# The MLP products of a hybrid decoder layer, as seven-product block multiplications over two token halves

## What is computed

```python
    x = x + gt1 * mix
    h = _rmsnorm(x, g2n) * (1 + sc2) + sh2
    x = x + gt2 * (jnp.square(jax.nn.relu(h @ w_up)) @ w_down)
...
y_prompt = _rmsnorm(xp, g_final)
y_sample = _rmsnorm(xs, g_final)
```

## Time and profile before

| | us |
|---|---|
| median of 3 runs (1808.34 to 1810.19) | 1808.41 |
| span of the profiled execution | 1804.3 |
| TensorE busy (matmuls) | 1775.4 |
| VectorE busy | 759.9 |
| ScalarE busy | 489.3 |
| GpSimd busy | 12.3 |

### The profile page before, as it was taken

One profiled execution on the slowest core, in us unless ns is written; L12 is line 12 of the kernel. 1 busy time (PEld: TensorE's weight loads), 2 busy tenths in 40 slices (PEclk: granted clock), 3 DMA queues, 4 the chain that ended last, 5 costly groups with the idle time before them and its releaser, 6 DMA issues.

```text
span 1804.3 us, 26783 instructions
## 1 busy us (share of the span) xinstructions
PE 1775.4 (98%) x10976; PEld 1713.8 (95%) x10976; DVE 759.9 (42%) x1445; ACT 489.3 (27%) x832; POOL 12.3 (1%) x25
## 2 busy tenths in 40 slices
PE   8999999999999999999999989999999999999997
PEld 3899999999999999999999989999999999999997
DVE  3644324444544545333353564343333333433345
ACT  5443333223333233211232341212121121212122
POOL 0000000000000000000000010000000000000000
PEclk9999999999999999999999989999999999999999
DMA  9444544322331232211132111111111111111112
GB/s 310 141 138 156 176 130 131 83 60 69 88 97 54 63 98 58 58 47 46 49 88 79 47 36 47 48 48 46 46 37 45 46 46 46 46 46 46 47 47 97
DMA packets 192677, 139.34 MB, mean 77 GB/s; under 512 B 15323, under 2 KB 176007, under 8 KB 192630
## 3 DMA queue, kind: packets, MB, share of 16 engines
q1 hardware_dynamic: 185910, 130.01, 24.4%
q10 hardware_dynamic: 6720, 8.67, 1.4%
HBM read 120.86 MB, written 17.80 MB: 77 GB/s over the span
## 4 chain that ended last, share of the span: by engine, by line
PE 95%; DVE 2%; DMA 1%; issue 1%; ACT 1%; SPq 0%; DVEq 0%; ACTq 0%
PE PB L916 85%; PE M L844 3%; PE M L969 1%; PE M L860 1%; PE M L1044 1%; DMA araw<-in_w_ada 1%; PE M L1050 1%; PE M L1036 1%; PE M L1038 1%; DVE XL L1223 1%; PE M L908 0%; PE M L1014 0%; DVE R L1709 0%; ACT A L532 0%; PE M L1061 0%
## 5 line engine op out<-in xcount | busy, mean ns | idle before, releaser
L916 PE MATMUL PB<-XH,whi 128*128 128x352 f32 x2496 | 811.3, 325 | 4.1 <-DVE XL L1223 2.1
L916 PE MATMUL PB<-XH,wlo 128*128 128x352 f32 x2496 | 801.5, 321 | 0.0
L916 PE MATMUL PB<-XL,whi 128*128 128x352 f32 x2496 | 801.3, 321 | 0.0
L916 PEld LDWEIGHTS PB<-XH,whi 128*128 128x128 f32 x2496 | 469.0, 188 | 11.3 <-issue 6.9
L916 PEld LDWEIGHTS PB<-XL,whi 128*128 128x128 f32 x2496 | 470.2, 188 | 0.7
L916 PEld LDWEIGHTS PB<-XH,wlo 128*128 128x128 f32 x2496 | 468.7, 188 | 0.0
L550 ACT ACTIVATE whi<-raw 128x1024 fp32r<-128x1024 f32 x134 | 141.3, 1054 | 407.4 <-PE PB L916 404.3
L916 PE MATMUL PB<-AH,whi 128*128 128x352 f32 x720 | 233.1, 324 | 0.2 <-issue 0.2
L916 PE MATMUL PB<-AL,whi 128*128 128x352 f32 x720 | 232.5, 323 | 0.0
L916 PE MATMUL PB<-AH,wlo 128*128 128x352 f32 x720 | 232.1, 322 | 0.0
L1228 DVE TENSOR_TENSOR wlo<-raw,whi 128x1024 fp32r<-128x1024 f32 x134 | 163.7, 1222 | 118.0 <-ACT whi L550 117.1
(11 more groups left out here) (297 smaller groups left out, 1199.4 us busy)
## 6 DMA issues: line engine op xcount, KB each, us to landing
raw<-in_w_in SPq DMA_DIRECT2D x64, 512.0 KB, 4.8
araw<-in_w_ada SPq DMA_DIRECT2D x48, 512.0 KB, 5.3
raw<-in_w_up SPq DMA_DIRECT2D x32, 512.0 KB, 4.0
raw<-in_w_down SPq DMA_DIRECT2D x32, 512.0 KB, 3.4
zp_d<-zr ACTq DMA_DIRECT2D x16, 512.0 KB, 2.7
Z<-zp_d SPq DMA_DIRECT2D x8, 1024.0 KB, 5.8
xin<-in_x_prompt SPq DMA_DIRECT2D x8, 512.0 KB, 7.0
CU<-in_state_C SPq DMA_DIRECT2D x8, 512.0 KB, 3.8
```

Source lines behind the costliest of these rows:

```text
L916: ins = pe.matmul(PB[:, bank, 0:BLK], w[:, w0:w0 + P], x[:, k, a0:a1], start=(k == 0 and j == 0), stop=(k == n_k - 1 and j == 2))
```

## The change

Both products of the MLP become block multiplications of 2x2 blocks with seven products in place of eight, in Winograd's form with its shared sums. The blocks: two halves of the tokens (`HALF` = 528), two halves of the inner dimension, two halves of a strip of 256 output features.

- **Up**: 16 steps p, each for 256 hidden features: seven products of four k tiles, each with three matmuls for each of two quarters of 264 tokens (`SUB`), in two PSUM banks (`acc`). The two quarters alternate with the same weight tile. Four pairs of banks serve the seven products (`ACC`); three products accumulate on what another left.
- **Down**: 32 steps, four for each of 8 groups of 512 hidden features, seven products of two k tiles.
- **Weights**: of each step seven operands are split; three of them, and the seventh, are sums and differences of the raw blocks, four operations on GpSimd (`sums`, `last_sum`).
- **Combining**: VectorE adds the accumulators (`u2`, `v1`, `t22`, `t21`, `t12`), ScalarE copies the first out (`s1_copy`) and takes relu and square of the four blocks, 528 wide. For the down products four of their seven x operands are differences of the blocks: four chained subtractions on GpSimd (`x_sums`). All seven are split again (high on ScalarE, low on VectorE) and stored to DRAM (`xd_d`), 528 KB each, since they don't fit into SBUF; SyncE loads them again, fourteen for each group, while the group before is multiplied.
- **Norm**: all seven x operands of the up products must be made once, 28 pieces of 528 tokens. The sum of squares is taken by a matmul with a matrix of ones, so that it is spread at once, and the square root (ScalarE) and the reciprocal (VectorE) are taken of 352 columns. Products of step 0 run in the order `FIRST` and wait for their pieces. x itself is stored to DRAM in phase 4 (`xm_d`) and loaded again in the down stage.
- **End**: VectorE and GpSimd combine the halves in the last group; the nine groups of rows are transposed, normed and stored after the last product.

The core of the diff:

```diff
+HALF = T // 2
+SUB = HALF // 2
+LPH = TP - HALF
+UP, DOWN = 16, 32
+ACC = (0, 1, 2, 3, 0, 2, 3)
+XPOS = (1, 5, 4, 3, 2, 6, 0)
+FIRST = (0, 4, 2, 1, 3, 5, 6)
...
+    def acc(a):
+        return PS[:, 2 * a:2 * a + 2, 0:SUB]
...
+        def store_x(p, i, done):
+            sp.wait_ge(s["xl5"], 7 * p + done)
+            sp.dma_start(xd_d[bass.ds(p, 1), :, i + 1, :].rearrange("o p n -> (o p) n"),
+                         XS[:, XPOS[i]].rearrange("p x n -> p (x n)")).then_inc(xbo if done <= 3 else xto, 16)
+        def store_t(p):
+            store_x(p, 3, 4)
+            store_x(p, 2, 5)
+            store_x(p, 1, 6)
+            store_x(p, 5, 7)
...
+        def load_xd(g, b, i, free):
+            sp.wait_ge(s["pd5"], free)
+            sp.wait_ge(xbo, 48 * (2 * g + 2 if isinstance(g, int) else UP))
+            sp.wait_ge(xto, 64 * (2 * g + 2 if isinstance(g, int) else UP))
+            for k in range(2):
+                sp.dma_start(xd(b, i)[:, k].rearrange("p x n -> p (x n)").bitcast(F32),
+                             xd_d[bass.ds(2 * g + k, 1), :, i + 1, :].rearrange("o p n -> (o p) n")).then_inc(xdi[b], 16)
...
+        def up(p):
+            load_up(p + 1)
+            if not (isinstance(p, int) and p == 0):
+                store_t(p - 1)
+            store_b(p)
...
+        def sums(P0, a, s1, s2, free):
+            if free is not None:
+                pool.wait_ge(s["wl5"], free)
+            pool.tensor_tensor(s1, a(1, 0), a(1, 1), ALU.add).then_inc(s["sum5"], 1)
+            link("sum5", pool.tensor_tensor(a(1, 0), a(0, 0), a(1, 0), ALU.subtract), 4 * P0 + 2)
+            link("sum5", pool.tensor_tensor(s2, s1, a(0, 0), ALU.subtract), 4 * P0 + 3)
+        def last_sum(P0, a, s2):
+            pool.wait_ge(s["wl5"], 7 * P0 + 2)
+            pool.tensor_tensor(s2, a(0, 1), s2, ALU.subtract).then_inc(s["sum5"], 1)
...
+        def x_sums(p):
+            first = isinstance(p, int) and p == 0
+            pool.wait_ge(s["b5"], 4 * p + 4)
+            for j, (out, a, b) in enumerate(((TB1, B12, B11), (TB2, B22, B12), (TB3, B22, TB1), (TB4, B21, TB3))):
+                if not first:
+                    pool.wait_ge(s["xl5"], 7 * (p - 1) + 4 + j)
+                if j >= 2:
+                    pool.wait_ge(s["tt5"], 4 * p + 2 * j - 3)
+                pool.tensor_tensor(out, a, b, ALU.subtract).then_inc(s["tt5"], 1)
+        def up(p):
+            if not (isinstance(p, int) and p == 0):
+                x_sums(p - 1)
+            up_sums(p + 1)
+            up_last_sum(p + 1)
...
+        def relu2(p, n, buf):
+            act.activation(buf, buf, ACT.Relu).then_inc(s["rl5"], 1)
+            act.wait_ge(s["rl5"], 3 * p + n)
+            act.activation(buf, buf, ACT.Square).then_inc(s["b5"], 1)
+        def bhi(p, i, src, n=None):
+            if n is not None:
+                act.wait_ge(s["b5"], 4 * p + n)
+            if not (isinstance(p, int) and p == 0):
+                act.wait_ge(xbo if XPOS[i] < 3 else xto, (48 if XPOS[i] < 3 else 64) * p)
+            act.activation(XS[:, XPOS[i], 0, :].bitcast(F32R), src, ACT.Copy).then_inc(s["xh5"], 1)
...
+        def thi(p):
+            for j, (i, src) in enumerate(((3, TB1), (2, TB2), (1, TB3), (5, TB4))):
+                act.wait_ge(s["tt5"], 4 * p + j + 1)
+                bhi(p, i, src)
...
+            if not first:
+                up_hi(p, 6)
+                act.wait_ge(s["c12c"], p)
+                relu2(p - 1, 3, B12)
+                s1_copy(p, UB[:])
+                thi(p - 1)
+            w(0)
...
+            act.wait_ge(s["t22c"], p + 1)
+            if first:
...
+            bhi(p, 6, B22, 1)
+            for i in range(1, 4):
+                w(i)
+            act.wait_ge(s["pd5"], prod(p, 4))
+            if not first:
+                act.wait_ge(s["tt5"], 4 * (p - 1) + 1)
+            act.activation(two(B11), acc(0), ACT.Relu).then_inc(s["c11c"], 1)
+            act.wait_ge(s["c11c"], p + 1)
+            act.activation(B11, B11, ACT.Square).then_inc(s["b5"], 1)
+            bhi(p, 0, B11, 2)
+            w(4)
+            act.wait_ge(s["c21c"], p + 1)
+            relu2(p, 2, B21)
+            bhi(p, 4, B21, 3)
+            w(5)
...
+            pe.matmul(rms_psum(b), ones[:], SQA[:, a0:a1], start=True, stop=False)
+            pe.matmul(rms_psum(b), ones[:], SQ[:, a0:a1], start=False, stop=True).then_inc(s["rms_mm"], 1)
...
+            if (b, k) in ((1, 6), (2, 3)):
+                rms_sum(b - 1)
...
+        FREE = [("c11c", 0), ("u2c", 0), ("c21c", 0), ("c12c", 0), ("s1c", 1), ("v1c", 1), ("t22c", 1)]
+        def turn_of(P0, i):
+            pe.wait_ge(s["wl5"], 7 * P0 + i + 1)
+            name, n = FREE[i]
+            if not (isinstance(P0, int) and P0 + n == 0):
+                pe.wait_ge(s[name], P0 + n)
+        def part(i, k, w, x, n_k):
+            for j, (wx, xx) in enumerate(((0, 0), (0, 1), (1, 0))):
+                for u in range(2):
+                    ins = pe.matmul(acc(ACC[i])[:, u, :], w[wx], x[xx][:, SUB * u:SUB * u + SUB], start=(i < 4 and k == 0 and j == 0),
+                                    stop=(k == n_k - 1 and j == 2), skip_group_check=i >= 4)
+            return ins
...
+        with pe.Fori(1, UP) as p:
+            up(p)
...
+        def rstd(b):
...
+            dve.reciprocal(RSTD[:, a0:a1], RSTD[:, a0:a1]).then_inc(s["rstd_done"], 1)
...
+        def xlo(i, k):
+            dve.wait_ge(s["xh2"], x_count(i, k))
+            out, x, hi = XX[i][:, k, 1, :], x_src(i, k), XX[i][:, k, 0, :].bitcast(F32)
+            bias = x_bias(i, k)
+            if bias is None:
+                ins = dve.tensor_tensor(out, x, hi, ALU.subtract)
+            else:
...
+        def u2(p):
+            dve.wait_ge(s["s1c"], p + 1)
+            dve.wait_ge(s["pd5"], prod(p, 1))
+            dve.tensor_tensor(two(UB[:]), acc(1), two(UB[:]), ALU.add).then_inc(s["u2c"], 1)
...
+        def v1(p):
+            dve.wait_ge(s["u2c"], p + 1)
+            dve.wait_ge(s["pd5"], prod(p, 2))
+            if isinstance(p, int) and p == 0:
+                dve.wait_ge(s["hbp"], 3)
+            else:
+                dve.wait_ge(s["tt5"], 4 * (p - 1) + 3)
+            dve.tensor_tensor(two(B22), acc(2), two(UB[:]), ALU.add).then_inc(s["v1c"], 1)
...
+        def t22(p):
+            dve.wait_ge(s["v1c"], p + 1)
+            dve.wait_ge(s["pd5"], prod(p, 3))
+            dve.tensor_tensor(two(B22), acc(3), two(B22), ALU.add).then_inc(s["t22c"], 1)
...
+        def t21(p):
+            dve.wait_ge(s["pd5"], 7 * p + 6)
+            if not (isinstance(p, int) and p == 0):
+                dve.wait_ge(s["tt5"], 4 * p)
+            dve.tensor_tensor(two(B21), acc(2), two(UB[:]), ALU.add).then_inc(s["c21c"], 1)
...
+        def t12(p):
+            dve.wait_ge(s["pd5"], 7 * p + 7)
+            if not (isinstance(p, int) and p == 0):
+                dve.wait_ge(s["tt5"], 4 * (p - 1) + 2)
+            dve.tensor_tensor(two(B12), acc(3), two(UB[:]), ALU.add).then_inc(s["c12c"], 1)
...
+        def blo(p, i, src):
+            dve.wait_ge(s["xh5"], 7 * p + XPOS[i] + 1)
+            dve.tensor_tensor(XS[:, XPOS[i], 1, :].bitcast(F32R), src, XS[:, XPOS[i], 0, :], ALU.subtract).then_inc(s["xl5"], 1)
...
+            if not first:
+                t12(p - 1)
+                up_lo(p, 6)
+                blo(p - 1, 3, TB1)
+                blo(p - 1, 2, TB2)
+                u2(p)
+                blo(p - 1, 1, TB3)
+                blo(p - 1, 5, TB4)
+                v1(p)
+            w(0)
+            if not first:
+                t22(p)
+            blo(p, 6, B22)
+            for i in range(1, 4):
+                w(i)
+            blo(p, 0, B11)
+            t21(p)
+            w(4)
+            blo(p, 4, B21)
+            w(5)
```

More of the change, by code:

```diff
@@ new lines, in _ @@
+        down(0, 0)
+        down(1, 1)
+        with sp.Fori(1, 3) as t:
+            down(2 * t, 0)
+            down(2 * t + 1, 1)
+        down(6, 0)
+        sp.wait_ge(s["pd5"], 7 * (UP + 27) + 2)
+        for h in range(2):
+            sp.dma_start(X2[:, 4 * h:4 * h + 4, :], xm_d.rearrange("k p n -> p k n")[:, 4 * h:4 * h + 4, HALF:T]).then_inc(s["x2_in"], 16)
+        down(7, 1, last=True)
+        sp.wait_ge(s["wl5"], 7 * (UP + DOWN))
+        sp.dma_start(GF[:], I["g_final"].rearrange("(o n) -> o n", o=1).broadcast_to([P, D])).then_inc(s["x2_in"], 16)
@@ L504, in layer_kernel @@
+        down(0)
+        down(1)
+        with pool.Fori(1, 3) as t:
+            down(2 * t)
+            down(2 * t + 1)
+        down(6)
+        down(7, last=True)
     POOL_STEPS = 11
@@ new lines, in _ @@
+        down(0, 0)
+        down(1, 1)
+        with pe.Fori(1, 3) as t:
+            down(2 * t, 0)
+            down(2 * t + 1, 1)
+        down(6, 0)
+        down(7, 1)
+        pe.wait_ge(s["s1c"], UP + DOWN)
+        for r, (t0, n) in enumerate(Y_GROUPS):
+            if r in (0, 3):
+                pe.wait_ge(s["c21c" if r == 0 else "c12c"], UP + DOWN)
+            if r >= 4:
```

(64 more changed lines are left out.)

905 lines of the change are left out of this document (520 added, 385 removed).

## The result

The changed kernel takes **1867.12 us** (median of 4, 1862.62 to 1870.42) against 1808.74 for the kernel before (1808.34 to 1810.19): ratio 1.0321, 95% interval 1.0301 to 1.0340. It is slower by 3.2%, 52 us above the forecast of 1815.2 and 22 above the end of the range.

The account below looks back on a forecast made before the run. TensorE's matmul time was taken to bound the kernel. Terms of -92.2 + 16 + 44 + 18.4 + 18.9 + 1.7 = +6.8 on a span of 1804.3 gave 1811.1, plus 4.1 around it: 1815.2 us, range 1770 to 1845.

Parts of the forecast that it names:

- Matmuls: In the MLP, 5376 matmuls of 264 columns at 0.120 us replace 4608 of 352: a gain of 92.2 us.
- The last out product: Before the MLP: block 2 waits 2 us for the second square; the product ends at 1033.6, 1 us earlier.
- Boundary: Between out products and up: reciprocals, scalings, low parts and subtractions on VectorE and GpSimd delay step 0, +16 us.
- Up: Up steps 1 to 15: rounds of 22.8 us where matmuls need 20.2, +44 us.
- The ring: In up steps, a chain through VectorE, ScalarE and GpSimd queues sets the round: 20.8 us without meetings, 22.8 taken.
- the clash: GpSimd and VectorE exclude one another on SBUF operations; full meetings lengthen an up round from 20.8 to 23.3 us.
- rival D: Up rounds last 25 us because of hand-overs by register waits: 1846 us in total, slower; chance 20%.
- Up to down: Between up and down: TensorE waits for the first group's operand loads from DRAM, +16.4 us, and 2 for the clock.
- Down: Down stage: TensorE binds at 10.1 us a step, with stops for late loads and the last group's additions, +18.9 us.
- the six stops: In down groups, a weight load queued behind 7.57 MB lands late: 1.1 us x 6, none at 435 GB/s.
- Tail: After the last product: nine groups of final rows remain, 20.5 us, +1.7 us against before.
- A: The likeliest case: helper engines' ring with clashes, as summed; 1803 to 1830 us, chance 50%.

Follow-up runs that it names:

- experiment 3: The changed kernel with the MLP matmuls of each k tile ordered quarter by quarter, so no weight tile is used twice in a row: 1861.25 us.
- Experiment 7: experiment 1 and experiment 2 together with earlier first-group loads, plus GpSimd's fifteen operations before and in step 0 moved to VectorE: 1765.93 us, ratio 0.9759.
- experiment 1: The changed kernel with VectorE's order in the up steps changed, t21, t12, v1 and t22 taken earlier: 1819.91 us, ratio 1.0068.
- experiment 5: The changed kernel with GpSimd's weight sums in the up steps cut to 8 columns from step 1 on: 1838.83 us.
- experiment 6: The changed kernel in its old order, with the four chained x subtractions of each up step on VectorE instead of GpSimd: 1822.63 us.
- experiment 9: Experiment 7's kernel with the operand loads of the first down group cut to half: 1761.56 us.
- experiment 2: The changed kernel with the next group's fourteen operand loads spread over the down group's steps, behind each step's weight load: 1821.21 us, ratio 1.0070.
- kernel 8: Experiment 7's kernel with each product of the first down group waiting for its own operand's loads instead of all fourteen: 1764.92 us, ratio 0.9755.

## Why the prediction was wrong, point by point

The direction was right, the size wrong by 51 us, on a span forecast at 1811.1 and measured at 1862.3. The direction had been given 0.52: 92 us of gain and 99 of losses nearly cancelled, so that it came out owes something to luck.

- **Matmuls: right.** 168 in 20.25 us, 0.1206 each for the 0.120 taken, and 5376 of them. The weight load hides, and experiment 3 says that the alternation has no part in it. The estimate that went with the Trainium skill's gap (TensorE: Matmul & The Clock Gate, Back-to-back issue gap) was 112.5 ns; the rows show 120.6. The Trainium skill calls it the gap of a single, isolated matmul there, and these are streams with a weight load ahead of each.
- **The start: not the change's.** The first out product begins 4.7 us later than before. The kernels are the same up to there; TensorE's clock was half for a part of two early stretches (0.83 in 18 to 34 us, 0.89 in 82 to 98), and in the ten experiments this start lay from 0.6 us earlier to 2.2 later than in the kernel before. The prediction had no term for it. The two windows of the changed kernel:

```profile
18.00:34.00 16.00, 15.67 (x72) 9.12 (x72) 5.52 (x17) 7.87 (x12) 0.00 (x0) 0.83 1.05 366
...
82.00:98.00 16.00, 14.05 (x76) 13.39 (x75) 4.58 (x6) 5.17 (x8) 0.00 (x0) 0.89 0.61 194
```

- **The last out product: wrong by 3.8.** It was to end 1 us sooner. From the first to the last matmul the out products take 2.8 us longer than before. TensorE waits 1.51 and 1.54 us for the squares, and the all-ones matmuls take 1.02 us behind each wait (1038.35 to 1039.37). But some 1.6 of the 2.8 is the clock, half for a part of the first out product: the first row is of the changed kernel, the second of the kernel before, at about the same place of its work. In the seven experiments whose clock stayed full there the out products took 0.1 to 1.3 us longer than in the kernel before, in the three others 2.4 to 2.8.

```profile
930.00:945.00 15.00, 13.16 (x76) 12.89 (x75) 12.47 (x12) 10.19 (x12) 0.00 (x0) 0.89 0.12 37
...
925.00:940.00 15.00, 13.16 (x86) 12.89 (x85) 12.70 (x13) 10.19 (x12) 0.00 (x0) 1.00 0.16 49
```

- **Boundary: 76.1 us from the last out matmul to the first v1 for 72.2 forecast.** The reciprocal of 352 columns was put at 2.7 us and takes 2.35. The clashes with GpSimd cost a little more than taken: every one of the twelve subtractions takes 1.8 us, and the low part beside it as long; the last low part of step 0 ends 54.2 us after the out products, for 50.4 forecast, and from there to v1 it is 21.6 as forecast. Experiment 7 shows that taking them away gains 4 us here, so the mechanism was right.
- **Up: 23.2 for 22.8**, 5.5 us in all. The ring, its members and their order were right, and so was the clash; experiments 1, 5 and 6 each break or shorten it as the sum of its parts says. No row has a price for the quarter of a microsecond at each hand-over by which rival D was longer, and a round of 23.2 leaves no room for eight of them. What was left out: behind five of the fourteen stops the clock was half for a while (0.83 from 1300 to 1310, below), and the stop ahead of the next v1 is then 1.2 to 1.4 us instead of 2.7. The ring hid the clock's loss.

```profile
1300.00:1310.00 10.00, 7.32 (x50) 7.14 (x49) 7.71 (x10) 5.55 (x10) 6.91 (x5) 0.83 0.49 199
```

- **Up to down: 17.5 for 16.4.** Right in size and cause; experiment 9 shows that most of such a hole is bytes.
- **Down: 375.9 us between the first and last matmul for 341.5 + 2 of clock. This is the step that failed: 32 of the 51 us.** The mechanism was named (weights queued behind 7.57 MB of operands), but its terms were mis-sized. First, the stop of a group was put at 1.1 us, by which the load would be late. It was 2.5 to 3.8 us late, as ScalarE's waits for it show (1643.18 above, and another group here), and each time TensorE's stop is some 0.2 us shorter than that wait:

```profile
1596.31 0.42 ACT L1053 ACTIVATE WHL<-WR 128x256 fp32r<-128x256 f32 x1 [3.81 <-DMA WR<-in_w_down]
```

  The load took 14.8 to 15.2 us in the six groups rather than 13.0, which is the difference between 1.1 and the mean stop of 2.9. The three sums, the split and VectorE's queue, 4.9 us from the landing to the next matmul, carry the delay to TensorE; they add nothing to it, for where the load is in time (experiment 2) the same operations hold nothing up. Six stops of 2.4 to 3.6 us are 17.2 for 6.6; group 0 had 13.9 for 8.3; the last group 4.7 for 4. Second, the half clock behind these stops (all of group 0's, and four of the six) was left out of the sum but for 2 us; it is 14 to 16. Experiment 2 takes away the six stops, 9 us of group 0's and some 10 of the half clock, and gets 37.6 us back; a stop of 4.7 us in group 0 and the last group's stay.

  The Trainium skill's ceiling of 435 GB/s (DMA: Bandwidth & Descriptors, Specifications), by which the six stops were to go, was not reached: the window from 1620 to 1640 has 385 with the DMA engines busy all the time, near the 375 taken, and the stops stayed.
- **Tail: 20 us for 20.5.** Right. The median lies 4.8 us above the profiled span for the 4.1 taken; 1.7 of it is around the span, the rest is that the profiled execution was 3.1 us faster than the median.
- **Rivals.** A's mechanism was the case, but the time is 37 us above its own range of 1803 to 1830, and the whole range closed too low, since no case had a larger loss in down than the likeliest one. That the ring could be left behind by a mere order of the queues was in none of them.

## What to carry to other kernels

When an algorithm takes work off the engine that binds, write down the ring that the helper engines form through their in-order queues, from a buffer's release to the next, and compare its length, not their busy share, with the time of the step: here four engines at 93%, 55%, 36% and 21% gave a step 15% above the matmuls', and four additions taken earlier in VectorE's queue made the step the matmuls' own 20.25 us. Spread bulk loads behind the small urgent ones instead of issuing them in one block. And charge every stop of TensorE twice, once for itself and once for the half clock that may follow it: here 16 us beside 36 of stops.

The version with both orders, earlier loads and the boundary on VectorE (kernels 7 and 8) takes 1765 us, 2.4% less than the kernel before: the seven-product form pays once its round is the matmuls' and no load is late. It is not at its end. In kernel 7, 70 us pass from the last out matmul to the first product 5 of step 1, for 288 matmuls that need 35, and the hole between up and down costs 16.
